# A diffusion trunk kernel on one core: six of the eight first modulation vectors move from a block of their own into norm 1 and the first projections

## The chip, the core and the metric

The kernel runs on one core of one Trainium2 chip. The time is device microseconds from the start of the program to its end. TensorE is called PE here (PEld is its weight load), VectorE DVE, ScalarE ACT, GpSimd POOL and SyncE SP. SP computes nothing: it issues the weight transfers, one after the other, and waits before each until its slot is free. POOL issues the transfers of tokens, biases, gains and modulation rows.

## What is computed

Two layers over 640 tokens (5 tiles of 128, T = 5) with 1024 channels. The part that matters here stands at the start of each layer:

```python
mod_ctx = (jax.nn.silu(c_ctx) @ w_mod[l] + b_mod[l])[None, None, :]
mod_lat = (jax.nn.silu(c) @ w_mod[l] + b_mod[l])[:, None, :]
...
shift1, scale1, gate1, shift2, scale2, gate2 = jnp.split(mod, 6, axis=-1)
h = rms_norm(x, lp["g_norm1"]) * (1 + scale1) + shift1
mixed, ctx_t = token_mixing(h, lp, lam_init, ctx)      # first: u = h @ lp["w_in"]
x = x + gate1 * mixed
h = rms_norm(x, lp["g_norm2"]) * (1 + scale2) + shift2
x = x + gate2 * expert_choice_ffn(h, lp["w_router"], lp["w_e_gate"], lp["w_e_up"], lp["w_e_down"])
```

A modulation vector is one sixth of `mod`: 1024 numbers for each of two conditions, out of a 1024 x 1024 piece of `w_mod`. Layer 0's norm 1 needs only two of them, shift1 and scale1 of layer 0. The attention of four branches (A, B, C, D) and a mixture of 16 experts follow; they are not touched.

## The kernel before, in words

Every weight is used in three matmuls: it is split into a high part (rounded to a shorter type, by ACT, `split_high`, L1179) and a low part (the rest, by DVE, `split_low`, L1548), and so is the activation. Weights come in chunks through a ring of 8 slots (`ring`, 512 KB each) that SP fills in the order of use. A slot comes free when PE has used the chunk (`ring_used`); there are 4 slots for high parts, so ACT's split of a chunk waits until PE has used the fourth one before it.

The program starts with a block for the eight modulation vectors in `FIRST` (six of layer 0, two of layer 1). Per vector there are 8 chunks of 128 rows x 1024 columns of `w_mod`, 64 chunks in all (`CH_MOD`). For each, PE multiplies four times (L744, L745, L747): two halves of 512 columns, low and high. After 8 chunks ACT copies the sums out (`mod_evac`), PE adds the partial rows and the bias (`mod_tail`, L757: two matmuls in float32, each shown as two instructions), DVE writes the row (`mod_copy`), and POOL stores it to DRAM (`mod_store`). Everything has two buffers: `modrow`, `modsum`, and the bias transfer `bias_in`.

After the third vector POOL reads shift1 and scale1 back, spread over 128 partitions (`mod_in`, four transfers of 512 KB). Norm 1 of a token tile is then: `rms` on ACT (L1216), `stats` on DVE (reciprocal, L1617, L1619), `norm_turn` on PE (8 transposes, L725), `norm_highs` on ACT (L1182) and `norm_lows` on DVE (L1553).

Then come the projections of `STREAM`: D (416 columns), Aq (256), Akv (512), each for 5 tiles, each tile in four quarters `kq` of 6 matmuls (L530, L531, L532). D follows the norm tile by tile; beside Aq, DVE works on the small norms of branch D (squares, variance, rope, scaling); beside Akv PE turns the result (`ct`) and projects it (`qm`, L865), and DVE copies and rotates it. All engines follow an order written out by hand; waits are counters. In the changed kernel `modrow`, `bias_in` and the bank that `mod_tail` writes are single, and the order of all this work in layer 0 is one list, `EARLY`, that every engine walks through.

## Time and profile before

| what | us |
|---|---|
| median of 3 runs | 2872.6 (2867.6 to 2874.0) |
| the profiled execution | 2874.5 |
| its span in the trace | 2872.5 |
| PE busy | 2667.7 (93%) |
| DVE busy | 1931.0 (67%) |
| ACT busy | 1628.8 (57%) |
| POOL busy | 471.6 (16%) |
| start of the first projection matmul | 125.6 |
| end of Akv and the last `qm` | 203.0 |

The profiled execution is 1.9 us above the median; 2.0 us of it lie outside of the span. PE is busy for 93% of the time, but the stretches differ: the first 125 us are the only ones before the experts in which the 16 DMA engines are busy all the time, and only there and in the attention does PE have gaps. A "granted clock" of 1.00 is TensorE's upper level, 2.4 GHz, and 0.50 the lower one, 1.2 GHz. PE's busy time in a stretch with the lower level counts slow work as busy.

### The profile page before, as it was taken

How to read it: one execution, taken by the hardware profiler on the slowest of the kernel's cores; microseconds unless marked ns; L12 is line 12 of the kernel's file. 1: busy time of each engine (PE TensorE's matmuls, PEld its weight loads, DVE VectorE, ACT ScalarE, POOL GpSimd, SP SyncE). 2: the span in 40 equal slices, each digit the busy share in tenths (PEclk: the TensorE clock that was granted, in tenths of full speed). 3: DMA queues.
4: the chain of work that ended last, by engine and by line, in shares of the span. 5: the costliest groups of instructions: out<-in, count | busy, mean ns of one | idle time of the engine just before them, and what ended most of it. 6: DMA issues, size and time to landing. Idle time of an engine off the chain costs nothing.

```text
span 2872.5 us, 40449 instructions
## 1 busy us (share of the span) xinstructions
PE 2667.7 (93%) x13576; PEld 1841.2 (64%) x13576; DVE 1931.0 (67%) x2986; ACT 1628.8 (57%) x2399; POOL 471.6 (16%) x359
## 2 busy tenths in 40 slices
PE   7898998989999999999989899899999799999995
PEld 1486676767774666666658666676777366666663
DVE  7743566435357999999955356643435799999995
ACT  7535544445224777777743554444522477777774
POOL 1030001212311121211003000031121112111221
PEclk9899999999998999999999999999999899999998
DMA  9630111212347999999972111121234599999995
GB/s 372 236 92 30 34 38 56 63 37 74 140 175 255 378 379 379 381 379 378 384 261 75 47 34 38 37 81 37 67 125 153 211 375 382 377 376 377 382 383 190
DMA packets 191184, 593.75 MB, mean 207 GB/s; under 512 B 23629, under 2 KB 33675, under 8 KB 191055
## 3 DMA queue, kind: packets, MB, share of 16 engines
q1 hardware_dynamic: 171646, 527.68, 49.6%
q0 software_dynamic: 19408, 64.37, 7.6%
q8 instruction: 79, 1.29, 0.2%
q14 instruction: 51, 0.41, 0.0%
HBM read 566.73 MB, written 25.23 MB: 206 GB/s over the span
## 4 chain that ended last, share of the span: by engine, by line
PE 76%; DVE 10%; ACT 6%; issue 5%; DMA 3%; ACTq 0%; POOL 0%; SPq 0%; DVEq 0%; POOLq 0%
PE bank L530 21%; PE bank L532 20%; PE bank L531 20%; PE bank L941 3%; PE bank L969 3%; PE bank L956 2%; ACT high L1179 2%; DVE low L1548 2%; DVE st L1857 1%; DMA ring<-in_w_mod 1%; PE bank L725 1%; DMA U<-x_normed,idx_g 1%; PE bank L1090 1%; PE bank L1128 1%; DVE sigr L1775 1%
## 5 line engine op out<-in xcount | busy, mean ns | idle before, releaser
L1179 ACT ACTIVATE high<-ring 128x1024 fp32r<-128x1024 f32 (+1 forms) x976 | 1023.1, 1052 | 387.0 <-PE bank L532 357.0
L1988 DVE TENSOR_TENSOR low<-ring,high 128x1024 fp32r<-128x1024 f32 x736 | 880.4, 1220 | 72.7 <-ACT high L1179 70.0
L530 PE MATMUL bank<-high,hT_high 128*128 128x512 f32 (+2 forms) x1280 | 518.8, 405 | 35.0 <-ACT U L1266 12.3
L531 PE MATMUL bank<-low,hT_high 128*128 128x512 f32 (+2 forms) x1280 | 487.1, 381 | 0.0
L532 PE MATMUL bank<-high,hT_low 128*128 128x512 f32 (+2 forms) x1280 | 486.2, 380 | 0.0
L530 PE MATMUL bank<-high,xeT_high 128*80 128x512 f32 x1056 | 419.3, 397 | 5.6 <-issue 3.5
L531 PE MATMUL bank<-low,xeT_high 128*80 128x512 f32 x1056 | 416.9, 395 | 0.0
L532 PE MATMUL bank<-high,xeT_low 128*80 128x512 f32 x1056 | 416.9, 395 | 0.0
L1548 DVE TENSOR_TENSOR low<-ring,high 128x1024 fp32r<-128x1024 f32 (+2 forms) x240 | 287.6, 1219 | 117.3 <-ACT high L1179 115.6
L530 PEld LDWEIGHTS bank<-high,hT_high 128*128 128x128 f32 x1280 | 244.3, 191 | 101.6 <-ACT sigr L1276 18.8
L1402 ACT ACTIVATE att<-bank,st 128x640 f32<-128x640 f32 (+3 forms) x200 | 136.6, 683 | 300.5 <-DVE st L1862 244.7
L532 PEld LDWEIGHTS bank<-high,hT_low 128*128 128x128 f32 x1280 | 243.9, 191 | 46.9
L531 PEld LDWEIGHTS bank<-low,hT_high 128*128 128x128 f32 x1280 | 245.0, 191 | 34.8
L530 PEld LDWEIGHTS bank<-high,xeT_high 128*80 128x80 f32 x1056 | 156.8, 149 | 90.3 <-issue 5.4
L532 PEld LDWEIGHTS bank<-high,xeT_low 128*80 128x80 f32 x1056 | 156.9, 149 | 87.5 <-issue 1.2
L531 PEld LDWEIGHTS bank<-low,xeT_high 128*80 128x80 f32 x1056 | 157.3, 149 | 83.0 <-issue 0.9
L530 PE MATMUL bank<-high,hidT_high 128*80 128x512 f32 x480 | 190.1, 396 | 8.9 <-DVE hidT_low L1553 8.9
L1857 DVE TENSOR_REDUCE st<-bank 128x1 f32<-128x640 f32 (+3 forms) x200 | 136.5, 682 | 87.0 <-PE bank L941 84.6
L2268 POOL DMA_INDIRECT x_resid<-oTr,idx_s x32 | 81.6, 2549 | 686.1 <-DVE oTr L1963 636.3
L531 PE MATMUL bank<-low,hidT_high 128*80 128x512 f32 x480 | 189.1, 394 | 0.0
L532 PE MATMUL bank<-high,hidT_low 128*80 128x512 f32 x480 | 188.8, 393 | 0.0
L2259 POOL DMA_INDIRECT U<-x_normed,idx_g x32 | 139.1, 4345 | 269.0 <-issue 109.0
(261 smaller groups left out, 3195.0 us busy)
## 6 DMA issues: line engine op xcount, KB each, us to landing
ring<-in_w_e_gate SPq DMA_DIRECT2D x256, 512.0 KB, 6.1
ring<-in_w_e_up SPq DMA_DIRECT2D x256, 512.0 KB, 7.0
ring<-in_w_e_down SPq DMA_DIRECT2D x256, 512.0 KB, 6.7
ring<-in_w_mod SPq DMA_DIRECT2D x64, 512.0 KB, 6.8
ring<-in_w_gate SPq DMA_DIRECT2D x64, 512.0 KB, 4.9
ring<-in_w_in SPq DMA_DIRECT2D x24, 512.0 KB, 4.2
U<-in_w_mod SPq DMA_DIRECT2D x20, 512.0 KB, 5.2
ring<-in_w_branch SPq DMA_DIRECT2D x16, 512.0 KB, 7.2
```

The costliest lines, as they stand in the source:

```text
L530: nc.tensor.matmul(out, lhs[0], rhs_high, start=start, stop=False)
L531: nc.tensor.matmul(out, lhs[0], rhs_low, start=False, stop=False)
L532: return nc.tensor.matmul(out, lhs[1], rhs_high, start=False, stop=stop)
L941: ins = mm(ps[p % 2][:, col:col + w], qT[r0:r0 + rn, b, un["m"] * P:(un["m"] + 1) * P], kT[r0:r0 + rn, b, a:a + w], start=True, stop=True)
L969: ins = mm(bank(6, P, 2 * P)[HD * z:HD * (z + 1), :], v_src(un, kb), pT, start=(i == 0), stop=(i == len(kbs) - 1))
L1179: A(high[:, HSLOT[g], :, 0:w], ring[:, SLOT[g], :, 0:w], ACT.Copy).then_inc(high_done, 1)
L1402: A(prob[:, p % 4, 0:w], ps[p % 2][:, 0:w], ACT.Exp, bias=negm[:, p % 8:p % 8 + 1], scale=SCALE[un["br"]], accum_out=sm[:, p % 8:p % 8 + 1 ...
L1548: V.tensor_tensor(low[:, SLOT[g], :, 0:w], ring[:, SLOT[g], :, 0:w], high[:, HSLOT[g], :, 0:w].bitcast(F32), ALU.subtract).then_inc(low_dv ...
L1857: then(V.tensor_reduce(mx[:, c8:c8 + 1], S[:, 0:w], AX.X, ALU.max))
L1988: V.tensor_tensor(low[:, SLOT[ahead], :, :], ring[:, SLOT[ahead], :, :], high[:, HSLOT[ahead], :, :].bitcast(F32), ALU.subtract).then_inc( ...
L2259: pool.indirect_dma_start(out=xe[0:CAP, b, :], out_offset=None, in_=xn_dram, in_offset=bass.IndirectOffsetOnAxis(ap=idx_g[:, b, 0:1], axis ...
L2268: pool.indirect_dma_start(out=x_dram, out_offset=bass.IndirectOffsetOnAxis(ap=idx_s[:, e, 0:1], axis=0), in_=ybuf[0:CAP, e, :], in_offset= ...
```

## The change

The eight vectors are cut into 16 halves of 512 columns (`HALVES`), each with 4 chunks of 256 rows x 512 columns; chunks are still 512 KB, but a row of one is 2 KB instead of 4 KB. The first four halves (`AHEAD`: shift1 and scale1 of layer 0) go through the ring as before, 16 chunks. The other twelve, 48 chunks, get 4 slots of their own for raw data and low parts (`MOD_RAW`, in U, M and later att) and 3 for high parts (`MOD_HIGH`). They are spread by `EARLY`: 8 before the first projection, 15 within D (3 per tile), 10 within Aq (2 per tile), 15 within Akv (3 per tile). A `mod_tail` of one half follows every fourth. ACT and DVE split 3 chunks ahead of PE, SP loads 4 ahead.

Buffers shrink to make room: `modrow`, its bias and the tail's bank are single; the turned norm tile has 2 banks instead of 4; `ct` has 2 banks instead of 4 and `qm` one instead of two. POOL loads three of the five token tiles only after the first store, and its rotation of Akv comes after the last modulation row is stored. The diff's core:

```diff
-FIRST = [(0, 0), (0, 1), (0, 2), (0, 4), (0, 3), (1, 1), (0, 5), (1, 4)]
-CH_MOD = KD * N_FIRST
+FIRST = [(0, 0), (0, 1), (0, 4), (1, 1), (1, 4), (0, 2), (0, 3), (0, 5)]
+HALVES = [(l, s, h) for l, s in FIRST for h in range(2)]
+AHEAD = 4
+CH_MOD = AHEAD * NQ_MOD
+N_MOD = (N_HALF - AHEAD) * NQ_MOD
+MOD_RAW, MOD_HIGH = 4, 3
...
+def plan_early():
+    for m in (2, 3, 4):
+        mods(2)
+        out.append(("rms", m))
+    out.append(("stats", 0))
+    mods(2)
+    out.extend([("turn", 0), ("stats", 1)])
+    for m in range(T):
+        for kq in range(NQ):
+            if kq == 1 and m + 1 < T:
+                out.append(("turn", m + 1))
+            out.append(("dense", ("W", "D"), m, kq))
+            if kq == 1 and m + 2 < T:
+                out.append(("stats", m + 2))
+            if kq < 3:
+                mods(1)
...
+            def mod_fill(j):
+                if j >= MOD_RAW:
+                    sp.wait_ge(mod_used, j - MOD_RAW + 1)
...
+                sp.dma_start(mod_raw(j), mod_src(AHEAD + n, kq)).then_inc(mod_full[j % MOD_RAW], 16)
...
+                    for i in range(NQ):
+                        in_chunk(i)
+                    for j in range(MOD_RAW):
+                        mod_fill(j)
+                    for i in range(NQ, 2 * NQ):
+                        in_chunk(i)
+                    sp.dma_start(rope[:, :, :], k_rope.rearrange("(m p) n -> p m n", p=P)).then_inc(table_in, 16)
...
+                    small_loads()
+                    for what, *x in EARLY:
+                        if what == "mod" and x[0] + MOD_RAW < N_MOD:
+                            mod_fill(x[0] + MOD_RAW)
...
+            def mod_tail(n):
+                pe.wait_ge(mod_row, n + 1)
+                pe.wait_ge(bm_full, 16 * (n + 1))
+                if n:
+                    pe.wait_ge(sum_ready, n)
+                mm(bank(3)[0:2, :], pair_sum[:, :], modrow, start=True, stop=True).then_inc(mod_sum, 1)
...
+            for g in range(CH_MOD):
+                pe.wait_ge(low_dve, g + 1)
+                mod_part(g // NQ_MOD, g % NQ_MOD, high[:, g % HIGH, :, :], low[:, g % RING, :, :]).then_inc(ring_used, 1)
+                if g % NQ_MOD == 1 and g > NQ_MOD:
+                    mod_tail(g // NQ_MOD - 1)
...
+            def bias_in(n):
+                l, at = mod_cols(n)
+                if n:
+                    pool.wait_ge(mod_sum, n)
+                pool.dma_start(modrow[4:5, :], b_mod[l:l + 1, at:at + NW]).then_inc(bm_full, 16)
```

How it moves instructions is seen in three places. First PE, at the first projection matmul. Before:

```order
L745 MATMUL bank<-high,csT 4x512
L757 MATMUL bank<-U,pair_sum 2x512 x2
L725 MATMUL bank<-ident,att 128x128 x8
L757 MATMUL bank<-U,pair_sum 2x512 x2
L725 MATMUL bank<-ident,att 128x128 x8
L530 MATMUL bank<-high,hT_high 128x416
```

After (L868, L867, L870 are the chunk's matmuls, L852 the transposes, L887 a tail):

```order
L868 MATMUL bank<-mod_high_u_67,csT 4x512
L852 MATMUL bank<-ident,att 128x128 x8
L625 MATMUL bank<-high,hT_high 128x416
L626 MATMUL bank<-low,hT_high 128x416
L627 MATMUL bank<-high,hT_low 128x416
L625 MATMUL bank<-high,hT_high 128x416
L626 MATMUL bank<-low,hT_high 128x416
L627 MATMUL bank<-high,hT_low 128x416
L868 MATMUL bank<-mod_high_u_68,csT 4x512
L870 MATMUL bank<-mod_low_u_63,csT 2x512
L867 MATMUL bank<-mod_low_u_63,csT 2x512
L868 MATMUL bank<-mod_high_u_68,csT 4x512
```

All modulation matmuls stood ahead of the first projection; now four of them, and a tail and a turn, stand between its first and second quarter. Second DVE, at the first `stats`, the normalised token tile 0. Before:

```order
L1548 TENSOR_TENSOR low<-ring,high 128x1024 x8
L1595 SCALAR_TENSOR_TENSOR U<-bank,U 2x512 x2
L1605 RECIPROCAL st<-st 128x1
L1617 SCALAR_TENSOR_TENSOR att<-att,st,M 128x1024
L1619 TENSOR_TENSOR att<-att,oTr 128x1024
L1548 TENSOR_TENSOR low<-ring,high 128x1024 x2
```

After (L1780 is the low part of one of the 48 chunks):

```order
L1780 TENSOR_TENSOR mod_low_m<-M,mod_high_u_67 128x1024
L1772 SCALAR_TENSOR_TENSOR oTr<-bank,U 2x512
L1780 TENSOR_TENSOR mod_low_u_63<-U,mod_high_u_68 128x1024
L1787 RECIPROCAL st<-st 128x1
L1799 SCALAR_TENSOR_TENSOR att<-att,st,M 128x1024
L1801 TENSOR_TENSOR att<-att,oTr 128x1024
L1780 TENSOR_TENSOR mod_low_u_64<-U,mod_high_u_66 128x1024
L1780 TENSOR_TENSOR mod_low_u_65<-U,mod_high_u_67 128x1024
L1733 TENSOR_TENSOR hT_low<-bank,hT_high 128x4x128 x2
```

The first `stats` now stands behind the low part of the ninth of the 48 chunks (number 8, counted from 0), and the hT lows of tile 0 behind the numbers 9 and 10. Third SP's queue, at its start. Before:

```order
L588 DMA ring<-in_w_mod 128x1024 x64
L581 DMA ring<-in_w_in 128x2x416 x4
L654 DMA rope<-in_k_rope 128x4x192
L655 DMA mask_na<-in_k_mask_na 128x64
L656 DMA mask_sw<-in_k_mask_sw 128x256
```

After:

```order
L686 DMA ring<-in_w_mod 128x2x512 x16
L676 DMA ring<-in_w_in 128x2x416 x4
L695 DMA U<-in_w_mod 128x2x512 x3
L695 DMA M<-in_w_mod 128x2x512
L676 DMA ring<-in_w_in 128x2x256 x4
L769 DMA rope<-in_k_rope 128x4x192
L770 DMA mask_na<-in_k_mask_na 128x64
L771 DMA mask_sw<-in_k_mask_sw 128x256
```

The first four of the 48 chunks stand before the Aq weights; the tables and the 17 small loads follow, and only then the fifth chunk.

## Rows read from the trace of the kernel before

**Rows 1.** Busy time in four stretches: block, D, Aq, Akv.

```profile
core 0: us, PE busy (x) PEld busy (x) DVE busy (x) ACT busy (x) POOL busy (x), PEclk, DMA share, GB/s
0.00:125.60 125.60, 96.74 (x304) 25.34 (x305) 94.70 (x97) 85.12 (x102) 14.67 (x32) 0.87 0.93 347
125.60:152.00 26.40, 26.40 (x149) 25.95 (x148) 16.41 (x22) 10.47 (x22) 0.51 (x1) 0.98 0.10 28
152.00:167.00 15.00, 15.00 (x126) 14.68 (x125) 13.16 (x53) 5.71 (x11) 1.12 (x2) 1.00 0.39 132
167.00:203.00 36.00, 36.00 (x158) 27.87 (x157) 13.92 (x30) 11.57 (x34) 19.24 (x33) 1.00 0.16 49
```

**Rows 2.** The same view for three stretches inside the block.

```profile
27.00:32.00 5.00, 4.18 (x17) 1.24 (x16) 4.24 (x4) 4.78 (x6) 0.00 (x0) 0.91 1.03 409
87.00:92.00 5.00, 5.00 (x11) 1.08 (x10) 2.22 (x3) 2.94 (x5) 0.00 (x0) 0.50 0.78 274
112.00:117.00 5.00, 5.00 (x11) 1.06 (x10) 4.21 (x5) 1.06 (x2) 0.00 (x0) 0.50 0.79 266
```

**Rows 3.** ACT in order of time: start, duration, engine, line; chunks 7 and 15.

```profile
20.98 1.06 ACT L1179 ACTIVATE high<-ring 128x1024 fp32r<-128x1024 f32 x1 [1.50 <-DMA ring<-in_w_mod]
...
32.34 1.06 ACT L1179 ACTIVATE high<-ring 128x1024 fp32r<-128x1024 f32 x1 [0.23 <-DMA ring<-in_w_mod]
```

**Rows 4.** POOL's transfers by issue: count, size, us to landing; three stretches.

```profile
U<-in_b_mod POOLq DMA_DIRECT2D x1, 4.0 KB, 15.5
...
U<-in_b_mod POOLq DMA_DIRECT2D x1, 4.0 KB, 5.4
...
M<-mod_rows POOLq DMA_DIRECT2D x2, 512.0 KB, 9.8
oTr<-mod_rows POOLq DMA_DIRECT2D x2, 512.0 KB, 11.8
mod_rows<-U POOLq DMA_DIRECT2D x3, 8.0 KB, 5.1
```

**Rows 5.** SP's queue in order of time, from the first table on.

```profile
105.75 0.47 SPq L654 DMA_DIRECT2D rope<-in_k_rope  x1
...
116.34 85.77 SPq L581 DMA_DIRECT2D ring<-in_w_in  x16
```

**Rows 6.** The page's part on issues: us to landing of weight chunks.

```profile
ring<-in_w_mod SPq DMA_DIRECT2D x64, 512.0 KB, 6.8
ring<-in_w_gate SPq DMA_DIRECT2D x64, 512.0 KB, 4.9
```

**Rows 7.** Groups of ACT and DVE by form, 0 to 115 us: busy, mean ns.

```profile
L1179 ACT ACTIVATE high<-ring 128x1024 fp32r<-128x1024 f32 x64 | 66.0, 1054 | 26.0 <-DMA ring<-in_w_mod 23.3 <-PE bank L747 2.5
...
L1548 DVE TENSOR_TENSOR low<-ring,high 128x1024 fp32r<-128x1024 f32 x64 | 76.0, 1218 | 22.2 <-ACT high L1179 21.4
L1595 DVE SCALAR_TENSOR_TENSOR U<-bank,U 2x512 f32<-2x512 f32 x6 | 3.8, 671 | 0.0
...
L1617 DVE SCALAR_TENSOR_TENSOR att<-att,st,M 128x1024 f32<-128x1024 f32 x2 | 2.6, 1285 | 0.1
L1619 DVE TENSOR_TENSOR att<-att,oTr 128x1024 f32<-128x1024 f32 x2 | 2.4, 1224 | 0.1
```

**Rows 8.** Group of DVE by form, 125.6 to 203 us: hT lows.

```profile
L1553 DVE TENSOR_TENSOR hT_low<-bank,hT_high 128x512 fp32r<-128x512 f32 x8 | 5.1, 683 | 0.6 <-ACT hT_high L1182 0.6
```

**Rows 9.** PE in order of time: chunk matmuls, tails at either clock, turn, first projection.

```profile
28.36 0.39 PE L745 MATMUL bank<-high,csT 128*4 128x512 f32 x1
28.59 0.40 PE L744 MATMUL bank<-low,csT 128*2 128x512 f32 x1
...
35.91 1.87 PE L757 MATMUL bank<-U,pair_sum 5*2 5x512 f32 x4
...
84.89 3.57 PE L757 MATMUL bank<-U,pair_sum 5*2 5x512 f32 x4
...
118.61 1.97 PE L725 MATMUL bank<-ident,att 128*128 128x128 f32 x8
...
125.63 0.69 PE L530 MATMUL bank<-high,hT_high 128*128 128x416 f32 x1
...
130.82 1.04 PE L725 MATMUL bank<-ident,att 128*128 128x128 f32 x8
```

More of the change, by code:

```diff
@@ L190, with mods @@
 OT_M = [(0, 1), (2, 3), (4,)]
+def plan_early():
+    out, j = [], 0
+    def mods(n):
+        nonlocal j
+        for _ in range(n):
+            out.append(("mod", j))
+            if j % NQ_MOD == 0 and j:
+                out.append(("tail", AHEAD + j // NQ_MOD - 1))
+            j += 1
+    for m in (2, 3, 4):
[13 more added lines that the diff above has]
+                mods(1)
+    norm = [("square", m) for m in range(T)] + [("variance",)] + [("kpe", m) for m in range(TS)] + [("scaled", m) for m in range(T)]
+    for m in range(T):
+        for kq in range(NQ):
+            out.append(("dense", ("W", "Aq"), m, kq))
+            if kq % 2:
+                mods(1)
+            if norm:
+                out.append(norm.pop(0))
+    for m in range(T):
+        out.append(("ct", m))
+        if m == T - 1:
+            out.append(("ct", T))
+        if m:
+            out.append(("qm", m - 1))
+        for kq in range(NQ):
+            out.append(("dense", ("W", "Akv"), m, kq))
+            if kq < 3:
+                mods(1)
+        if m == 2:
+            out.append(("lambda",))
+    out.extend([("qm", T - 1), ("tail", N_HALF - 1)])
+    return out
+EARLY = plan_early()
+MOD_TURN = sum(1 for x in EARLY[:EARLY.index(("dense", ("W", "Aq"), 0, 0))] if x[0] == "mod")
 def plan_uses():
@@ L457, in hybrid_step @@
         mod_out = [sem(f"mod_out{i}") for i in range(2)]
[L458 removed]
+        g_row_in = [sem(f"g_row_in{i}") for i in range(2)]
         ones_set, later_b = sem("ones_set"), [sem(f"later_b{i}") for i in range(2)]
@@ L2131, in _ @@
                     pool.wait_ge(xe_tr, 2 * NE * l)
-                for m in range(T):
+                for m in range(T if l else 2):
                     pool.dma_start(xt1[:, m, :], tok_in(l, m)).then_inc(x_in[m], 16)
```

512 lines of the change are left out of this document (308 added, 204 removed).

## Prediction, made before the changed kernel ran

> **What bounds the kernel now.** I read the busy time by stretch first. The block of 64 chunks takes 125.6 us, with the DMA engines at 0.93 of their time and PE at 96.7 us of busy time, part of it at the lower clock. Then PE is busy without a gap for 77.4 us: D 26.4, Aq 15.0, Akv 36.0 [rows 1]. So the block is bound by transfers and by what follows them, and D to Akv by PE alone, while ACT needs 10.5, 5.7 and 11.6 us there, DVE 16.4, 13.2 and 13.9, and the DMA engines are nearly idle. That is the room. Inside the block the engines move 409 GB/s at a full share, but 266 to 274 GB/s in two late stretches in which PE stands at clock 0.50 and is busy all the time [rows 2]: there PE is what is waited for. The time can change only up to the end of Akv, 203.0 us; behind it the same instructions follow in the same order. POOL's rotation of Akv moves from beside Akv (POOL has 19.2 us of work in that stretch [rows 1]) to after it. It is for branch A, and the twenty attention units of branch D come first, so I cost it at nothing; were D's attention not there to cover it, it would be those 19 us.
>
> So I need two numbers: when the first projection starts (125.6 before), and how long PE takes from there to the end of Akv (77.4 before).
>
> **What a chunk costs.** ACT 1.05 us, DVE 1.22 [rows 7]. PE issues a chunk's matmul every 0.23 us at the upper clock, four of them 0.92; a tail of a whole vector took 1.87 at the upper clock and 3.57 at the lower, so one of a half is 0.93 or 1.8 [rows 9]. DVE's copy of a half is 0.67 [rows 7]. Landing takes 4.9 us for a chunk with 2 KB rows beside little else, 6.8 for one under full load [rows 6]. The work's amount does not change (64 chunks, 16 half tails for 8 whole ones); its place does.
>
> **First term: the start of the first projection.** Two chains lead there, and I walk both in this order.
>
> The 16 first chunks. Before, chunk 15 was split at 32.3 us [rows 3], after 16 chunks (8.4 MB) and five token tiles (2.6 MB). Now only two of the token tiles and about half of the other three are ahead of it: 1 MB less, 2.5 us at 409 GB/s. Against that, rows are halved to 2 KB. The nearest row with shorter runs is the stretch of the small loads, 266 GB/s at a share of 0.79, 337 at a full one, and the 4 KB rows of the chunks give 409 [rows 2]. So 8.4 MB take 20.5 to 24.9 us; I take the middle, 2.2 more. Chunk 15 comes at about 32.
>
> The Trainium skill has a rule against this edit (Perfetto Trace Analysis, DMA Optimizations): small transfers below 2 KB carry a noticeable overhead each, and batching 2 KB to 4 KB or 8 KB can improve throughput a lot. By it the chunks would go at the slow end. The stretch of small loads agrees in direction, and its 337 against 409 GB/s puts a price of 4.4 us on it at most.
>
> The bias. `modrow` is single, so a bias is asked for only when the tail before is done, and the next tail waits for it. A bias took 5.4 us to land from an empty POOL queue and 15.5 us behind five token tiles [rows 4]. The first tail stands behind chunk 7, which comes some 1.5 us sooner than the 21.0 before [rows 3]: split, copy and a tail at the lower clock end it at 22.5. Bias 1 lands at 28.5, tail 1 ends at 29.5; bias 2 stands behind three token tiles, between the two landings: their 1.6 MB at half of 409 GB/s end at about 35, which I take. PE holds chunk 14 back for that tail: tail 2 at 36, chunk 15 used at 39, bias 3 at 42, tail 3 at 43, DVE's copy at 44.5.
>
> Chain one, the modulation rows: the store lands in 5.1 us and the rows come back in about 9.8 [rows 4], with issue at 58 to 60. Alone it would let the first `stats` start there.
>
> Chain two, SP's queue: the last Aq chunk needs the slot of chunk 15, 39 us. Behind it stand the tables and small loads, 20 issues in 10.6 us (105.75 to 116.34) [rows 5]. So the fifth of the 48 chunks is asked for at 50 and lands at 55.5. ACT, DVE and PE use it by 58.5, and that frees the slot for the ninth, which lands at 64 (both between 4.9 and 6.8 [rows 6]). On DVE the first `stats` stands behind the ninth chunk's low part: 66.2. Then `stats`, 2.65 with its reciprocal [rows 7], ends at 69, the turn takes 1.0 to 2.0 [rows 9], and DVE's lows of the tenth and eleventh chunk (2.4) and of tile 0 (1.3 [rows 8]) end at 72.5. Chain two is last. **The first projection starts at 72.5 instead of 125.6**, with 66 as the lower bound (chain one decides) and 79 as the upper (bias 2 later, 6.8 us for each landing).
>
> **Second term: from there to the end of Akv.** PE had 77.4 us. Added: 40 of the chunks at 0.92, 36.8; 11 half tails at 0.93, 10.2; the turn of tile 1, which stood before the start, 0.9. Sum 125.3. The start at the lower clock is in the 26.4 already, and stays. Is another engine later? In D PE needs 9.3 us a tile; DVE needs a `stats` 2.65, two lows 1.35, three chunks 3.7, a copy 0.5, together 8.2. Covered, by 1.1 us. In Aq PE needs 15.0 + 9.2 + 2.8 = 27. DVE had 13.2 in that stretch [rows 1] and gets 12.2 for ten chunks, 2.0 for copies, and more of Akv's four lows (about 2.6 of them fell behind the stretch): 30. So I add 3, between 0 (PE has chunks split ahead) and 6. In Akv PE needs 54, DVE 13.9 + 18.3 + 2.7 = 35: covered. ACT has more room everywhere. The single banks for turn, `ct` and `qm` add waits on work that is finished several us before PE asks, as each tile now takes PE longer: nothing. Were that cover gone, a turn would wait for one hT low, 1.3 us.
>
> Sum: 72.5 + 125.3 + 3 = 200.8, against 203.0. **The start moves 53 us up, and 51 of them are given back.** The profiled execution took 2874.5 us; less 2.2 this is 2872.3. The median was 1.9 below the profiled time, so the median becomes 2870.4, and I predict **2870 us**.
>
> **Rivals.**
> 1. *SP's queue is not last.* If the biases and the ring let chunk 15 go at 33 instead of 39, chain two is 6 us earlier and both chains end at 66; if DVE's 3 us in Aq are absorbed too, it is 66 + 125.3 = 191.3, 11.7 less: 2861. For it: a bias takes only 5.4 us where nothing stands ahead of it [rows 4]. Against it: three tiles ahead of bias 2 are fixed by the order.
> 2. *Slower: the four raw slots.* A slot is refilled when PE has used it. The loop is issue 0.4, landing, ACT 1.05, DVE 1.22, PE 0.92, and DVE may be in a `stats` (2.65) when the chunk comes. At 4.9 us it is 11.1. Four chunks take PE 12.4 us in D and 10.8 in Aq, so it begins to decide in Aq at once by 0.3, and in D from a landing of 6.2. At 7.5 it is 13.7: 1.3 / 4 x 15 = 5 us in D, 2.9 / 4 x 10 = 7 in Aq, instead of my 3: 9 more, 2879, and with a start two us later 2881. For it: 6.8 us is the median of the w_mod chunks now. Against it: that is under full load, and here a chunk every 3 us asks for 175 GB/s.
> 3. *The clock.* Each short wait of PE inside the mix could bring the lower clock, as the waits of the block did (0.50 in two stretches [rows 2]). Five more us of work at it, in two or three places, is 5 to 8 us: 2877. Since PE is busy nearly always there, small.
> 4. *It does not do what it says*: the chunks' matmuls wait so that PE does them all after the projections. The order of PE is fixed, so it would need rival 2 at its worst; it has no chance of its own.
>
> **Chances.** Forecast 0.48, rival 1 0.27, rival 2 0.17, rival 3 0.08. A change of this kernel's time can be told from none beyond about 0.2%, 5.7 us: below 2866.9 or above 2878.3. The forecast's own range is 2865 to 2876 (bounds of the two terms that do not reach the rivals); about 0.07 of its 0.48 lie below 2866.9. Rival 2 lies above and half of rival 3: faster 0.34, same 0.45, slower 0.21. The range reaches to rival 1 and most of rival 2: 2859 to 2881.
>
> **What would show it.** The first D matmul near 72 us, PE's idle time before it between 40 and 50 us, SP issuing the fifth of the 48 chunks near 50, DVE's first `stats` waiting for a chunk's high part and not for the modulation rows. In D to Akv PE busy at clock 1.00, with gaps only in Aq that end on DVE, and the first attention matmul at about 201 plus what follows now. If PE shows gaps in D that end on DVE's low, or ACT waits for raw chunks there longer than PE's slack, rival 2 is right. If `stats` starts before 62, rival 1. I am wrong in both terms if the block's DMA rate at 2 KB rows is well outside of 337 to 409 GB/s, or if PE's share of the mix is not the sum of its parts.

## The result, and the profile after

| | before | after |
|---|---|---|
| median of 20 runs each | 2871.65 us (2863.38 to 2875.59) | 2882.59 us (2872.56 to 2888.77) |
| the profiled execution | 2874.51 us, span 2872.5 | 2880.82 us, span 2879.0 |
| first projection | 125.6 | 78.6 |
| end of Akv | 203.0 | 209.3 |
| from there to the end of the span | 2669.5 | 2669.7 |

The changed kernel is **slower**: ratio 1.0041, 95% interval 1.0033 to 1.0048, about 10.9 us. The forecast was 2870 us, level with before, in a range of 2859 to 2881; the measured median lies 1.6 us above that range. The start of the projections came forward by 47 us, and 53 were given back. All of the difference between the two traces lies ahead of the end of Akv.

Busy time by stretch, as in [rows 1]: the head, then D, Aq and Akv with the chunks between their pieces.

```profile
core 0: us, PE busy (x) PEld busy (x) DVE busy (x) ACT busy (x) POOL busy (x), PEclk, DMA share, GB/s
0.00:78.50 78.50, 41.89 (x114) 10.73 (x114) 44.51 (x48) 44.60 (x60) 13.26 (x29) 0.76 0.89 313
78.50:121.90 43.40, 43.35 (x206) 29.68 (x207) 33.35 (x37) 22.18 (x30) 5.08 (x10) 0.96 0.55 166
121.90:150.00 28.10, 26.00 (x162) 18.42 (x162) 22.84 (x61) 13.56 (x20) 2.55 (x5) 1.00 0.73 235
150.00:209.50 59.50, 59.19 (x252) 35.81 (x251) 37.70 (x61) 32.44 (x57) 5.18 (x10) 1.00 0.58 175
```

PE is busy 43.35 of 43.40 us in D, 26.0 of 28.1 around Aq and 59.2 of 59.5 behind it. The mix (D to Akv with the chunks in it) is bound by PE, as forecast. In the head it is busy for 41.9 of 78.5, and the engines move 313 GB/s instead of the 347 of [rows 1]. The chain of waits (start, duration, what) says what came last there:

```profile
41.63 0.47 SPq L769
...
51.41 0.43 SPq L744
51.85 0.04 issue
51.89 9.06 DMA U<-in_w_mod
60.98 1.06 ACT mod_high_u L1357
62.06 1.24 DVE mod_low_u L1780
63.30 0.04 issue
63.34 0.59 PE bank L868
...
70.53 4.42 DMA U<-in_w_mod
74.98 1.06 ACT mod_high_u L1357
76.07 1.01 DVE mod_low_u L1780
77.08 0.14 issue
77.21 1.29 DVE hT_low L1733 x2
78.50 0.04 issue
78.55 0.71 PE bank L625
```

This is the prediction's chain two up to the fifth chunk: ahead of the first row PE used chunk 15 at 41.2 (forecast 39), then come twenty issues on SP, the fifth chunk, its split and its matmuls. Behind them the chain differs in one link. The prediction had the refill of the ninth chunk there; that one took 3.6 us, and the first `stats` stood behind it, from 71.2. The refill at 70.53 is the eleventh chunk's, whose low part came last in front of the lows of tile 0. The step that is far off is the line at 51.89: **9.06 us of landing where I had 5.5**. The transfers issued from 50 to 54 us show why (count, size, median us to landing):

```profile
U<-in_w_mod SPq DMA_DIRECT2D x3, 512.0 KB, 9.9
M<-mod_rows POOLq DMA_DIRECT2D x2, 512.0 KB, 6.5
oTr<-mod_rows POOLq DMA_DIRECT2D x2, 512.0 KB, 7.5
M<-in_w_mod SPq DMA_DIRECT2D x1, 512.0 KB, 11.4
```

Four refills and POOL's four broadcasts of the modulation rows are asked for within four microseconds, from 50.06 on. That is 4.2 MB, and at the 400 GB/s that the view by stretch gives for 50 to 61 us they need 10.5 us by themselves; with the small loads asked for just before, the last of them (the `M` line, the eighth chunk) landed at 64.8. In the mix the 36 refills land in 3.8 to 4.4 us (medians by buffer), so rival 2 did not happen at its size.

PE in order of time, with every wait from the first turn to the end of Akv:

```profile
74.02 1.09 PE L852 MATMUL bank<-ident,att 128*128 128x128 f32 x8 [2.02 <-DVE att L1801]
...
78.55 0.71 PE L625 MATMUL bank<-high,hT_high 128*128 128x416 f32 x1 [3.44 <-DVE hT_low L1733]
...
130.03 0.39 PE L625 MATMUL bank<-high,hT_high 128*128 128x256 f32 x1 [2.10 <-DVE low L1728]
...
153.25 1.02 PE L887 MATMUL bank<-oTr,pair_sum 5*2 5x512 f32 x2 [0.31 <-ACT oTr L1348]
```

The first two rows stand before the mix or at its start. Two waits, 2.4 us, stand inside the mix of 130.7. The larger is at the change from D to Aq. ScalarE waits 2.4 and 1.6 us there for chunks that have not landed (three refills asked for from 118.5 to 123.8, beside weights, took 5.3 to 5.8 us), and its splits of Aq's weights stand behind them in its queue, so DVE's low of the last weight chunk comes late (ScalarE in order of time):

```profile
123.92 1.06 ACT L1357 ACTIVATE mod_high_a<-U 128x1024 fp32r<-128x1024 f32 x1 [2.41 <-DMA U<-in_w_mod]
124.88 0.62 ACT L1328 ACTIVATE high<-ring 128x512 fp32r<-128x512 f32 x1
127.06 1.06 ACT L1357 ACTIVATE mod_high_a<-U 128x1024 fp32r<-128x1024 f32 x1 [1.56 <-DMA U<-in_w_mod]
```

The traces account for 6.3 of the 10.9 us. The other 4.6 lie between the profiled executions and the medians: before's stood 2.9 above its median, after's 1.8 below.

### The profile page after: what moved, and what is told of

The parts are those of the page before. It is cut to its first block, busy times and chain, and to the rows that moved or that the text cites. A ratio compares the mean times of both kernels' runs of the same rounds, so it can differ in the third digit from the quotient of the medians.

```text
span 2879.0 us, 40505 instructions
## 1 busy us (share of the span) xinstructions
PE 2662.7 (92%) x13576; PEld 1840.1 (64%) x13576; DVE 1928.7 (67%) x2986; ACT 1628.8 (57%) x2399; POOL 460.6 (16%) x379
## 4 chain that ended last, share of the span: by engine, by line
PE 76%; DVE 10%; ACT 5%; issue 5%; DMA 3%; SPq 1%; POOL 0%; ACTq 0%; DVEq 0%; POOLq 0%
PE bank L625 21%; PE bank L627 20%; PE bank L626 20%; PE bank L1090 3%; PE bank L1118 3%; PE bank L1105 2%; DVE st L2074 2%; ACT high L1328 2%; DVE low L1728 1%; PE bank L868 1%; PE bank L867 1%; PE bank L926 1%; PE bank L852 1%; DMA U<-x_normed,idx_g 1%; PE bank L1239 1%
## 5 line engine op out<-in xcount | busy, mean ns | idle before, releaser
L1328 ACT ACTIVATE high<-ring 128x1024 fp32r<-128x1024 f32 (+1 forms) x928 | 974.3, 1051 | 373.4 <-PE bank L627 358.2
L1728 DVE TENSOR_TENSOR low<-ring,high 128x1024 fp32r<-128x1024 f32 (+2 forms) x192 | 231.3, 1220 | 102.6 <-ACT high L1328 101.3
L2467 POOL TENSOR_TENSOR M<-M,sigr 128x512 f32<-128x512 f32 x60 | 102.5, 1728 | 402.8 <-DVE sigr L1992 402.8
```

Of the source, the lines that this page charges most:

```text
L1328: A(high[:, HSLOT[g], :, 0:w], ring[:, SLOT[g], :, 0:w], ACT.Copy).then_inc(high_done, 1)
L1728: V.tensor_tensor(low[:, SLOT[g], :, 0:w], ring[:, SLOT[g], :, 0:w], high[:, HSLOT[g], :, 0:w].bitcast(F32), ALU.subtract).then_inc(low_dv ...
L2467: G.tensor_tensor(dst, dst, sig[:, m, :], ALU.add).then_inc(g_add, 1)
```

## Experiments

Ratios are to the kernel before, run on the same chip; 0.001 is 2.9 us. F is the first projection matmul, E the end of Akv, in the profiled execution. "Low" is where the granted clock stands at 0.50 (1.2 of 2.4 GHz) after F.

| kernel | F | E | low after F | median, us | ratio, 95% interval |
|---|---|---|---|---|---|
| after | 78.6 | 209.3 | to 82 | 2882.6 | 1.0041 (1.0033, 1.0048) |
| after again | 75.9 | 209.5 | to 85 | 2881.6 | 1.0039 (1.0026, 1.0053) |
| small loads late | 76.3 | 206.8 | to 79 | 2880.1 | 1.0029 (1.0019, 1.0040) |
| biases early | 78.2 | 211.8 | to 87 | 2884.5 | 1.0044 (1.0028, 1.0061) |
| both | 73.9 | 211.6 | to 86, 130 to 137 | 2877.2 | 1.0017 (1.0005, 1.0028) |
| after, PE kept busy | 78.9 | 212.1 | to 87 | 2881.8 | 1.0030 (1.0021, 1.0038) |
| after, half of PE's chunk work | 74.9 | 200.8 | to 83, 125 to 135, 151 to 155 | 2873.3 | 1.0003 (0.9994, 1.0011) |
| 3 chunks ahead of the statistics | 65.7 | 206.5 | to 70, 118 to 124 | 2871.9 | 0.9995 (0.9985, 1.0006) |
| and none in D's last tile | 64.5 | 202.6 | to 68 | 2873.2 | 1.0007 (0.9997, 1.0017) |
| the same again | 63.9 | 204.0 | to 68, 122 to 129 | 2874.7 | 1.0013 (1.0003, 1.0022) |
| 1 chunk ahead | 61.7 | 209.3 | to 62, 69 to 72, 127 to 130, 151 to 154 | 2878.5 | 1.0029 (1.0015, 1.0043) |
| the same, with 55 transposes | 63.0 | 208.1 | 70 to 77 | 2879.4 | 1.0024 (1.0013, 1.0034) |
| the order of 1 chunk ahead in the kernel after | 65.4 | 209.5 | to 66, 72 to 76, 130 to 134 | 2879.9 | 1.0032 (1.0019, 1.0044) |
| 1 chunk ahead, second statistics first | 62.5 | 198.7 | to 63 | 2868.8 | 0.9992 (0.9983, 1.0000) |
| and the tails one chunk later | 61.7 | 199.4 | to 62, 121 to 124 | 2868.9 | 0.9991 (0.9982, 0.9999) |

**SP's queue and the biases.** The first edit puts the small loads behind the refills:

```diff
+                        if what == "mod" and SMALL_AT <= x[0] < SMALL_AT + 10:
+                            small_loads(x[0] - SMALL_AT)
```

> The kernel after, with the two mask tables, the rotation table and the 17 small loads issued on SP two at a time behind the sixth to fifteenth of the 48 chunks' issues, not in one block ahead of the fifth. Theory A (the start of the projections hangs on SP's queue: in the kernel after the fifth chunk was issued at 51.9 and landed 9.1 us later): the fifth chunk is issued at about 47.6, as soon as PE has used the first of the slots, lands by 54, and the first projection comes at 70 to 73 instead of 78.6; the time falls by 5 to 8 us. Rival B (the modulation rows' way back, or the bias of the tails, sets the start): the fifth chunk comes earlier but the first projection stays within 2 us of 78.6, and the time is the same within 2 us. Rival C (the late small loads hold up the start of the statistics or the chunks behind them): the first projection is later than 78.6.

The fifth chunk was issued at 49.0, when PE had used its slot, 2.9 us sooner; it landed 8.8 us later, beside the broadcasts as before. F moved by 2.3 and E by 2.5 us, and the time by about 3, but the ratio's interval overlaps that of after, and a second trace of after (below) has its F at 75.9 without any edit. So neither theory is shown: the queue did let the chunk go earlier (A), it was followed at once by the slot, and the burst stayed; the gain of 3 us is not clear of noise.

The second loads four biases at the start, each into its own row:

```diff
-        modrow = oTr[0:5, 2048:2560]
+        modrow_of = lambda n: sigr[0:5, n * NW:(n + 1) * NW] if n < AHEAD else oTr[0:5, 2048:2560]
...
-            bias_in(0)
+            for n in range(AHEAD):
+                bias_in(n)
```

> The kernel after, with the biases of the first four halves loaded at the start, each into a row buffer of its own, so that no tail of the first four waits for a bias issued behind the tail before it. Theory A (bias 2, issued at 29.3 and landed at 36.7, holds PE back from the last chunks of the first 16, and by their slots the last Aq chunk and SP's small loads): tail 2 moves from 36.7 to about 34, chunk 15 is used at 38 instead of 41, and the fifth of the 48 chunks is issued at 48 to 49 instead of 51.9; first projection 3 to 4 us earlier, the time 3 to 4 us less. Rival B (the modulation rows or the transfer rate set these times and the bias is covered): no change within 1 us.

Chunk 15 was used at 37.3 instead of 41.2, and all of it was lost on SP: the issues from there to the small loads (the rest of Aq, the tables) took 5.5 us where they took 2.3, and the fifth chunk was issued at 51.9 as in after. F came 0.3 us earlier, and the time is the same within the intervals: rival B's result, though not its reason, since the bias did move PE.

> Both edits together: small loads issued late, biases of the first four halves loaded early. Theory A (SP's queue and the bias lie on the same chain, one behind the other): first projection at 67 to 70 instead of 78.6, the time 9 to 12 us less than the kernel after, which is the kernel before within 2 us. Rival B (behind SP's queue stands at once the modulation rows' chain, ready at 58 to 60): the two gains do not add, the first projection stays at 72 or later and the time falls by 6 us or less.

Together F came at 73.9, 4.7 us earlier, and the time fell by about 7 us (1.0041 to 1.0017). F fits rival B, and the time lies between the two; the ratio's interval ends below that of after, so this gain is clear of noise. In the traced execution E did not come earlier at all: the clock stayed at 0.50 for 12 us after F and fell again at 130, behind PE's wait of 2.25 us between D and Aq:

```profile
74.00:84.00 10.00, 10.00 (x27) 5.96 (x28) 6.61 (x8) 2.25 (x3) 1.52 (x3) 0.50 0.20 58
84.00:129.00 45.00, 43.25 (x216) 30.38 (x214) 31.46 (x35) 24.00 (x33) 4.07 (x8) 0.98 0.78 241
129.00:137.00 8.00, 7.50 (x25) 4.07 (x26) 6.93 (x23) 2.50 (x3) 1.01 (x2) 0.57 0.44 145
```

The columns are those of [rows 1]. PE is busy in the whole of the first stretch and yet gets half the clock; in the 24 us before it, it was busy for 10.6.

**The same kernel a second time.**

> The kernel after once more, unchanged, for a second trace and times beside those of the other three. Theory A (the granted clock at the start of the mix and behind its one wait differs from one execution to the next, and that is why the median of after stood 10.9 us above before's while the two profiled executions differ by 6.3): first projection within 1 us of 78.6, the end of Akv within 3 us of 209.3, and, where it differs, a stretch at clock 0.50 in the mix that the first trace did not have; median 8 to 11 us above before. Rival B (the start differs between executions by more than the clock, such as a landing): first projection off by more than 1.5 us, with the clock the same.

F came 2.7 us earlier. The burst says why. Here the fifth chunk was asked for at 50.98, 1.0 us ahead of the first broadcast and not 1.8 behind it, and it landed in 4.8 us, at 55.8: as forecast. Transfers issued from 50 to 56 us:

```profile
U<-in_w_mod SPq DMA_DIRECT2D x3, 512.0 KB, 6.0
M<-mod_rows POOLq DMA_DIRECT2D x2, 512.0 KB, 9.1
oTr<-mod_rows POOLq DMA_DIRECT2D x2, 512.0 KB, 10.3
M<-in_w_mod SPq DMA_DIRECT2D x1, 512.0 KB, 12.6
```

The eighth chunk, the last asked for, took 12.6 us and landed at 65.4, and on ScalarE and DVE the ninth stands behind it: its low part started at 68.5, the first `stats` at 69.6 (forecast 66.2), and the steps from there to F took 6.3 us as forecast. So a fifth chunk in time did not save the start; the burst as a whole delays it, and what is asked for last in it lands last (65.4 here, 64.8 in the first trace). The run with half of PE's chunk work, below, has the same picture: the fifth chunk landed at 56.0, the eighth took 12.0, and F is 74.9.

E came at the same time, since the clock held 0.50 until 85, three microseconds longer than in the first trace. From 78 to 86, first the trace above, then this one:

```profile
78.00:82.00 4.00, 3.46 (x10) 2.31 (x10) 3.07 (x4) 0.00 (x0) 0.00 (x0) 0.52 0.00 0
82.00:86.00 4.00, 4.00 (x21) 2.29 (x20) 2.38 (x3) 2.14 (x3) 0.73 (x2) 1.00 0.39 132
```

```profile
78.00:82.00 4.00, 4.00 (x8) 0.69 (x7) 1.26 (x2) 1.06 (x1) 0.00 (x0) 0.50 0.21 35
82.00:86.00 4.00, 4.00 (x16) 3.48 (x16) 3.39 (x6) 1.19 (x2) 1.52 (x3) 0.56 0.28 101
```

So neither theory holds whole. F does differ between executions, by a landing (against A), and the clock is not the same (against B). One trace of such a kernel carries 2 to 3 us of this on either term, and the differences in F of that size in this table show nothing by themselves.

**Keeping PE busy.** Sixty transposes between the fourth and the fifth of the 48 chunks:

```diff
+        if m == 3:
+            out.append(("fill", FILL))
...
+                            for _ in range(x[0]):
+                                tr(bank(6, 0, P), ident[:, :], ident[:, :])
```

> The kernel after, with 60 extra 128x128 transposes on PE into a bank that nobody reads, put between the fourth and the fifth of the 48 chunks, where PE stood idle for 10.8 us (52.5 to 63.3). Eight such took 1.09 us at the upper clock, so they fill 8.2 of the 10.8 us there, or 14.8 at the lower. Nothing else is changed. Theory A (the lower clock, 0.50 from 54 to 81 but for 3 us, stretches the chain of the start): PE keeps the upper clock through chunks 5 to 10 and the first matmuls of the projections; the chain's tail and matmuls (7 us at the lower clock) shrink by 3 us, and the low-clock start of the mix by about 1.7 us; first projection 75 to 76 instead of 78.6, the time 4 to 6 us less than the kernel after. Rival B (the clock does not follow PE's work, or the chain hangs on transfers): same first projection and same time within 1.5 us. Rival C (the transposes run at the lower clock and end late): the fifth chunk's matmuls start after 63.3 and the time is up to 4 us more.

```profile
52.00:66.00 14.00, 10.91 (x75) 7.69 (x73) 3.53 (x3) 3.92 (x6) 2.12 (x4) 0.95 1.02 363
66.00:86.00 20.00, 14.43 (x39) 6.12 (x39) 14.86 (x17) 10.48 (x16) 2.04 (x4) 0.53 0.40 125
```

The clock followed PE's work: 0.95 from 52 to 66, where after has 0.52 from 54 to 66. But six waits, 0.4 to 2.8 us each, stood between 62 and F, and from 66 to 86 it was 0.53. F and E did not come earlier, and the ratio is 3 us lower with an interval that overlaps that of after. Rival B for F, and nothing shown for the time; its first reason (the clock does not follow) is refuted. Filling one gap does not help while others follow it.

**What PE's work in the mix is worth.**

```diff
-                    if kk:
+                    if kk and n < AHEAD:
                         mm(acc[0:2, :], csT[:, kk, 0:2], low_part[:, k, :], start=False, stop=False, skip_group_check=True)
```

(and the same for the first low part of a vector).

> The kernel after without the matmuls of the low parts of the 48 later chunks (two of four matmuls of each); transfers, splits and everything else as before, so the modulation vectors made late are less exact. Theory A (PE alone bounds the mix from the first projection to the end of Akv): 0.46 us less for each of the 37 chunks that stand in it, 17 us; plus about 4 us in the start, where eleven chunks run at the lower clock in front of the first projection, of which the transfers hide part: 17 to 21 us less than the kernel after. Rival B (the four raw slots or DVE are close behind PE): the waits of PE on splits grow from 2.4 us to 8 or more, and 8 to 12 us less than after.

The counts in that text were wrong: 40 chunks stand in the mix and eight before it. Summed over the mix, from each matmul's start to the next one's, the chunks' matmuls took 38.6 us in after and 21.5 here: 17.0 saved. The mix shrank from 130.7 to 125.9, 4.8 us. Of the 12.2 that are missing, PE's waits took 4.0 (6.4 against 2.4), the projections' own matmuls 5.4 (73.8 against 68.3), tails and turns the rest. The largest of the waits, and the two stretches at the low clock:

```profile
PE bank L625 <- DVE low L1728: 4.0, 2, 2.4
```

```profile
74.80:83.50 8.70, 8.64 (x24) 5.66 (x25) 6.14 (x10) 2.25 (x3) 1.53 (x3) 0.51 0.23 62
...
121.90:135.00 13.10, 11.43 (x43) 7.91 (x44) 9.64 (x27) 5.68 (x8) 1.02 (x2) 0.61 0.51 164
```

The projections got slower because of the clock: behind the waits at the end of D it is 0.61 over 13 us. The whole time fell by 9 us (11 by the ratios) where theory A asked for 17 to 21, and an F earlier by 3.7 is in it, of which the second trace of after has 2.7 without the edit. So rival B in the time, with waits of 6.4 us where it asked for 8 or more: DVE and the chunks' transfers stand close behind PE. What it lacked is the clock: **a wait here can cost its length and then the low clock that follows**.

**The shorter rows.** The kernel before with 2 KB rows:

```diff
-                sp.dma_start(ring[:, g % RING, :, :].rearrange("p h n -> p (h n)"),
-                             w_mod[l, k * P:(k + 1) * P, s * D:(s + 1) * D]).then_inc(ring_full[g % RING], 16)
+                sp.dma_start(ring[:, g % RING, :, :],
+                             w_chunk(w_mod[l], s * D + (k // 4) * NW, NW, k % 4)).then_inc(ring_full[g % RING], 16)
```

> The kernel before with one thing changed: each of the 64 modulation chunks is fetched as four blocks of 128 rows of 2 KB rather than 128 rows of 4 KB; the same bytes in all, the same slots and the same order of everything else. The contents land at other places, so the modulation vectors are other numbers. Theory A (the shorter rows move at a lower rate: 373 to 392 GB/s in the head of the kernel after against 409): the block, which takes 125.6 us and is bound by transfers for about two thirds of it, gets 3 to 8 us longer, and so does the time. Rival B (the rate is the same and the lower rate of after comes from what runs beside the chunks): no change within 1.5 us.

Ratio 1.0013 (1.0004 to 1.0022), 3.7 us for all 64 chunks; in the profiled execution the first projection stands at 127.4, 1.8 later. From 20 to 40 us, before and then with the short rows:

```profile
20.00:40.00 20.00, 16.79 (x54) 4.12 (x55) 16.31 (x14) 15.90 (x18) 0.00 (x0) 0.83 1.03 410
```

```profile
20.00:40.00 20.00, 16.04 (x53) 4.04 (x54) 16.85 (x14) 16.38 (x17) 0.00 (x0) 0.83 1.05 387
```

387 against 410 GB/s, 6% less: theory A, at its lower edge. On the 8.4 MB of the first 16 chunks that is 1.2 us, where I took 2.2. The Trainium skill's rule (Perfetto Trace Analysis, DMA Optimizations: transfers below 2 KB carry a significant overhead each, and batching 2 KB to 4 or 8 KB can help a lot), read for the rows of a transfer, has the right sign here; its size from 2 KB to 4 KB is these 6%.

**The order of the chunks.** If PE's idle time in the head is what is lost, fewer chunks should stand ahead of the first statistics. All of the following but one have the two edits from above. Three chunks ahead instead of eight (the text below counts the three that are split ahead of PE as well), four in each tile of Akv:

```diff
     for m in (2, 3, 4):
-        mods(2)
+        mods(1)
         out.append(("rms", m))
-    out.append(("stats", 0))
-    mods(2)
-    out.extend([("turn", 0), ("stats", 1)])
+    out.extend([("stats", 0), ("turn", 0), ("stats", 1)])
```

> The kernel with both edits, and a different order: only three of the 44 chunks of the later vectors stand before the first statistics and the first turn instead of eleven, and the last piece of Akv takes four chunks more to make up for it. Theory A (PE alone bounds the stretch from the first projection to the end of Akv, so that every microsecond in which it stands idle before the first projection is lost time): the first projection comes at 63 to 65, the total is 13 to 16 us below the kernel after and 2 to 5 us below the kernel before. Rival B (with so few chunks ahead DVE or the four raw slots decide inside the mix, and PE waits there for what it no longer waited for at the start): first projection at 63 to 65 too, but the mix is longer by 3 to 8 us than 130.7 us plus the moved chunks' share, and the total is no better than with both edits alone.

F at 65.7 and about 13 us less than after (1.0041 to 0.9995): theory A at its lower edge against after, but level with before instead of ahead of it. Rival B is right on the mix: it took 140.8 us, 5 more than 130.7 and the five moved chunks at 0.96 each. PE waits 3.2 us in it, and behind the wait at the end of D the clock fell to 0.50 from 118 to 124.

```diff
-            if kq < 3:
+            if kq < 3 and m < T - 1:
                 mods(1)
```

> The kernel with late small loads, early biases and the statistics first (3 chunks ahead of them), with one more change: the last tile of D has no chunks between its pieces, and three tiles of Aq have three instead of two. In the runs so far PE waits 1.9 to 2.3 us at the end of D for a split of Aq's weights that stands behind a chunk's split on ScalarE and DVE, and in two of five of them the granted clock fell to 0.50 for 7 us right behind that wait. Theory A: that wait goes (under 0.5 us), and with it the fall of the clock at 118 to 125: the mix is 3 to 5 us shorter than 140.8 us and the time 2 to 5 us below that of the order before (2871.9). Rival B (DVE is behind in Aq anyway): the wait reappears in Aq, 2 to 4 us of waits on splits there, and the time is the same within 1.5 us.

> The kernel with late small loads, early biases, three chunks ahead of the first statistics and a last tile of D without chunks, once more, for a second trace and for times beside the other two on the same chip. Theory A (it is level with the kernel before, as its times and those of the order before it said: 2873.2 and 2871.9 against 2872.5 and 2873.0): within 2 us of the kernel before. Rival B (its level times were luck with the clock in the mix): 4 us or more above before, with a stretch at clock 0.50 in the mix.

The wait at the end of D went, and smaller ones came in Aq: 3.5 us in the first trace, 2.5 in the second, which again shows a fall of the clock, behind a wait of 1.13:

```profile
122.00:129.00 7.00, 6.94 (x21) 3.59 (x22) 6.41 (x20) 3.35 (x5) 1.02 (x2) 0.52 0.34 96
```

Rival B of the first text. The second chip gave 1.0013, the first 1.0007; 3.6 us above before is between the second text's two theories, nearer to B.

**One chunk ahead.** ScalarE takes the splits three chunks ahead of PE. With three chunks ahead of the statistics it stood before the last sum of squares until the sixth chunk had landed (56.1). So:

```diff
-    for m in (2, 3, 4):
-        mods(1)
+    mods(1)
+    for m in (2, 3, 4):
         out.append(("rms", m))
-    out.extend([("stats", 0), ("turn", 0), ("stats", 1)])
+    out.extend([("stats", 0), ("turn", 0)])
+    mods(2)
+    out.append(("stats", 1))
```

> The kernel with late small loads, early biases and a last tile of D without chunks, with one more change of order: the three remaining token tiles' sums of squares, the first statistics and the first turn stand behind one chunk instead of three, and two chunks follow the turn. In the order before, ScalarE took the sixth chunk (landed at 56.1) ahead of the last sum of squares, and the chunks' refills shared the DMA engines with the four 512 KB broadcasts of the modulation rows, which took up to 12 us to land. Theory A (both set the start): the broadcasts land in 6 to 8 us, the first statistics start at 53 to 56 instead of 58.5, the first projection comes at 59 to 61 instead of 64.5, and the time is 3 to 6 us below the order before and 2 to 6 us below the kernel before. Rival B (what PE gains at the start it loses at once, since the chunks it has not done before the first tile come later with fewer of them split ahead): first projection at 59 to 61, waits of 2 us or more in the first tile of D, and the time within 2 us of the order before.

Theory A held for the start: with one refill beside them instead of three, the broadcasts landed in 5.9 and 7.9 us instead of 9.0 and 10.8 (medians of each pair). The 4.0 of the one refill is no gain: the first of the three took 4.2 before, as both were asked for ahead of the broadcasts. Transfers issued from 44 to 56 us, three chunks ahead, then one:

```profile
U<-in_w_mod SPq DMA_DIRECT2D x3, 512.0 KB, 9.4
M<-mod_rows POOLq DMA_DIRECT2D x2, 512.0 KB, 9.0
oTr<-mod_rows POOLq DMA_DIRECT2D x2, 512.0 KB, 10.8
```

```profile
M<-mod_rows POOLq DMA_DIRECT2D x2, 512.0 KB, 5.9
oTr<-mod_rows POOLq DMA_DIRECT2D x2, 512.0 KB, 7.9
U<-in_w_mod SPq DMA_DIRECT2D x1, 512.0 KB, 4.0
```

The statistics started at 53.9. But the time rose by 5 us (6 by the ratios), and PE's waits from 57 to 209 us (total, times, longest) say where it went:

```profile
PE bank L852 <- DVE att L1801: 4.8, 1, 4.8
PE bank L887 <- ACT oTr L1348: 3.2, 2, 2.1
```

The second turn waits 4.8 us for the second tile's statistics, which I had put behind two chunks on DVE.

> The same order, with 55 extra 128x128 transposes on PE into a bank that nobody reads ahead of the first turn, to fill 7.5 us of its idle time there at the upper clock. Theory A (the lower clock at the start of the mix comes from the idle time in front of it): the granted clock is 1.00 from the first turn on, the turn takes 1.0 instead of 2.0 us and the first 3 to 4 us of projections run at the upper clock; 2 to 3 us less than without them. Rival B (as with the 60 transposes put into the kernel after: the idle time that is left still brings the lower clock, only later): clock 0.50 in the first microseconds of D, no gain within 1 us.

With 55 transposes ahead of the turn the clock was 0.99 from 50 to 56 and 0.50 again to 62: rival B (F 63.0, and a ratio whose interval overlaps that without them).

> The kernel after with the new order of the chunks alone (one chunk ahead of the first statistics and turn, two behind the turn, none in the last tile of D, three in three tiles of Aq, four in each tile of Akv); small loads and biases as in the kernel after. Theory A (the order is what matters, since with it SP's queue no longer leads to the first projection; what leads there are the modulation rows): first projection at 61 to 64, the time 8 to 11 us below the kernel after, within 3 us of the kernel with all edits. Rival B (the late biases and the block of small loads still count): first projection at 66 or later, less than 7 us below the kernel after.

F at 65.4, ratio 1.0032 (1.0019 to 1.0044). It has the same 4.8 us wait, so it doesn't test its theories. Beside the run with one chunk ahead it says that in this order the two edits bring F 3.7 us and the time under 1.

Then the one line was moved:

```diff
-    out.extend([("stats", 0), ("turn", 0)])
+    out.extend([("stats", 0), ("turn", 0), ("stats", 1)])
     mods(2)
-    out.append(("stats", 1))
```

> The kernel with the three remaining sums of squares, the first statistics and the first turn behind one chunk, changed in one place: the second tile's statistics stand ahead of the two chunks behind the turn, not behind them. In the run before, PE waited 4.8 us in the first tile of D for the second turn, since DVE took the low parts of two chunks, the second landed at 63.9, ahead of those statistics; the first statistics themselves started at 53.9. Theory A (that one wait ate the earlier start): first projection at 61 to 62 as there, no wait above 1 us in the first tile of D, end of Akv 4 to 5 us earlier than the 209.3 of that run, and a time of 2872 to 2875, which is 4 to 6 us below it and about that of the order with three chunks ahead. Rival B (PE loses the same time in any order, since every chunk moved behind the start asks for its refill late): the wait moves to the low part of the fifth or sixth chunk, 3 us or more, and the time is within 2 us of the run before.

E at 198.7, 10.6 us earlier, and 9.7 us off the median (10.6 by the ratios, as the two ran on different chips): theory A, and more. The wait was 4.8 us; the trace of the run before also has 9 us at 0.50 behind its waits, and this one none. From F to E PE is at clock 1.00:

```profile
62.50:198.70 136.20, 133.17 (x640) 84.72 (x638) 100.87 (x162) 75.10 (x114) 14.32 (x28) 1.00 0.72 222
```

> The same with each of the eleven half tails inside the mix one chunk later on PE and DVE, so that ScalarE's copy out of the bank is over when PE comes to the tail (in the runs so far PE waits 0.3 to 2.1 us at some of the tails in Aq and Akv). Theory A: the waits on ScalarE at the tails (1.5 to 3 us in all) go to under 0.5, and the time is 1 to 3 us less than without. Rival B (the wait only shows ScalarE being late for its next split as well): they come back as waits on a chunk's low part, the time is the same within 1 us.

The waits on ScalarE at the tails went, two on lows (1.7 and 1.6 us) took their place, and the time stayed: rival B.

The last two are 0.08 and 0.09% faster than the kernel before, some 2.5 us, with intervals that end at 1.0000 and 0.9999. By the ratios they are 14 us faster than the kernel after.

## Why the prediction was wrong

- **Where the bound lies: right.** PE bounds D to Akv with the chunks in them, SP's queue and the transfers it asks for lead to the first projection, the rest of the kernel is untouched (2669.5 and 2669.7), and POOL's moved rotation costs nothing. The first projection came with PE idle for 36.6 us ahead of it, where the sign was 40 to 50.
- **The first 16 chunks and the biases: nearly right.** Chunk 15 was split at 32.5 (about 32), bias 2 landed at 36.6 (35), the tails ended at 22.0, 29.3, 38.2 and 43.9 (22.5, 29.5, 36, 43), and chunk 15 was used at 41.2 (39). By the run with 2 KB rows alone they cost 1.2 us of the head instead of 2.2.
- **The failed step: 5.5 us for a landing in the middle of a burst.** "It is asked for at 50 and lands at 55.5" was 51.9 and 60.9. The 5.5 came from rows with a full or light load of their own [rows 6]. I had both sides on the page: the refills "at 50" in chain two, the rows' way back "in about 9.8" in chain one. I walked the chains apart and never put their 4.2 MB side by side, and of the four refills I walked only the first. In the second trace of after that one landed at 55.8, as forecast, and the start was still 3.4 late, by the eighth chunk, which took 12.6. That the transfers share is shown from the other side too: with one refill beside them instead of three the broadcasts landed 3 us sooner.
- **The start: 78.6, not 72.5**, 6.1 late: 1.9 of issue, 3.6 of landing, and 0.6 in the 17 us behind it. These 0.6 are four things that nearly cancel: the fifth chunk's split and matmuls, at the low clock, took 1.3 more than forecast; the ninth chunk's landing 1.9 less (3.6 against 5.5); its split and low 0.2 more; and the lows of tile 0 came 1.0 late, since the eleventh chunk, whose landing the forecast left out, landed at 75.0.
- **The mix: 130.7, not 128.3.** The waits were 2.4 us, where I had 3 in about that place; they end on DVE as forecast, but ScalarE behind a late transfer makes them. The forty chunks took 38.6 instead of 36.8, and the projections 68.3 where the same matmuls of before sum to 66.9. About 1.0 of these 3.2 us is the low clock up to 82; the rest is small steps at the upper clock, 0.237 us from one chunk matmul to the next instead of 0.23, and 0.187 for a projection's instead of 0.184. The prediction said that the low-clock start "is in the 26.4 already": in before it ended 1.2 us behind the start of the first projection, here 3 us behind it, and 9 in the second trace.
- **Rival 3, the clock, stood in the wrong place.** I put it inside the mix at 0.08, for short waits. The two stretches that it names [rows 2] show no waits: PE is busy there all the time at 0.50. Both traces of after show the low clock mostly at the start, where PE comes out of 10.8 us of idle time (5.4 in the second), and none behind the wait in the mix. By an estimate from the first trace it is about 3 us of the 8.5 between forecast and trace (200.8 against 209.3): 1.0 in the fifth chunk's four matmuls, 1.0 by the eleventh chunk, whose slot PE freed late, and the 1.0 in the mix. The fifth chunk's landing is 3.6.
- **The last step: from the trace to the median.** The prediction took 1.9 us off the forecast for the profiled execution, since before's stood so far above the median of three runs. After's stood 1.8 below its median. So of the 12.2 us between 2870.4 and 2882.6, 6.1 are the start, 2.4 the mix and 3.7 this step; without it the median would have come out at 2878.9, inside the range. The step rested on one execution of before, and no row gave a reason for it.
- **4.6 us of the 10.9 between the two kernels** lie in no trace. The profiled execution of before stood high among its runs and that of after low. That the clock falls inside the mix in some executions of after would fit: it did in three of the eight traces that have the wait between D and Aq, and over the 20 runs of after the mean granted clock goes with the time, from 0.975 in the fastest (2872.6) to 0.970 and 0.969 in the two slowest (2888.8 and 2886.4). But neither trace of after shows it, so this stays open.

## What to carry to other kernels

When work is moved so that two chains start together, lay their transfers on one time axis and divide the bytes by the measured rate before giving either a landing time: eight 512 KB transfers asked for within four microseconds landed in 6.5 to 11.4 us by their medians, up to 12.6 in the second trace, where a refill in the mix took 3.8 to 4.4. Give each transfer of the burst a landing, the last one first. When filler work is put between pieces of a bound engine, check on each in-order queue (ScalarE and DVE here) what the next piece stands behind; one entry in the wrong order cost about 10 us, about what the whole change costs. Moving idle time out of the middle is worth less than it looks, since here the engine that came out of it ran at the lower clock for a while, so measure the gain at the end of the stretch and not at its start.

## What the runs showed of the hardware

The lower clock behind a wait of PE could cost as much as the wait or more: after 1.1 to 2.4 us of waiting in a stretch otherwise full, it stood at 0.50 for 3 to 10 us in seven traces, which is 1.5 to 5 us of lost work (an estimate, half of the stretch), and it did not fall in others with the same wait (2.10 in after, 2.18 with late small loads). The same kernel kept it at 0.50 until 82 us in one execution and 85 in another. A refill asked for 1.0 us ahead of four broadcasts landed in 4.8 us, one asked for 1.8 us behind the first of them in 9.1. Half of the chunks' matmuls taken away gave back 4.8 of 17.0 us in the stretch where they ran. Rows of 2 KB moved 6% slower than rows of 4 KB with all DMA engines busy.
